# Hybrid pooling and gating layer on eight cores: the first tile's transposed input made on chip, and loads and stores issued at other places

## The reference, cut to what matters

```python
# x: (32, 2048, 1024) float32
proj = einsum('bsd,dc->bsc', x, w_in)            # 512 pool columns | 512 u | 512 v
xp = proj[..., :512]
zg = gelu(proj[..., 512:])
pooled = causal_multiscale_pool(xp)              # 4 groups, trailing means over 2/4/8/16, minus x_t
pool_out = einsum('bsgc,gcd->bsgd', pooled, pool_w) * pool_scale
sgu_out = u * (W_s @ layer_norm(v) + b_s)        # chunks of 128 positions, lower-triangular W_s, 4 heads
mix = einsum('bsc,cd->bsd', concat(pool_out, sgu_out), w_out)
h = layer_norm(alpha * x + mix)
y = layer_norm(alpha * h + (silu(h @ w_gate) * (h @ w_up)) @ w_down)   # d_ff 2816
```

## Time and profile before

| | us |
|---|---|
| three runs | 2450.92, 2452.18, 2657.8 |
| their median | 2452.18 |
| the profiled execution's own time | 2450.96 |
| its span on the slowest core (core 3) | 2449.4 |
| spans of the eight cores | 2441.9 to 2449.4 |
| PE busy on that core | 2408.5 (98%) |

### The profile page before, as it was taken

How to read it: one execution, slowest core, us unless ns; L and a number is a source line. 1 busy time by engine, 2 the same in 40 slices (tenths; PEclk the granted TensorE clock), 3 DMA queues, 4 the chain that set the end, 5 groups by cost and what they waited for, 6 DMA issues and landing times.

```text
span 2449.4 us, 33772 instructions; the slowest of 8 cores (2441.9 to 2449.4 us)
## 1 busy us (share of the span) xinstructions
PE 2408.5 (98%) x11415; PEld 1101.7 (45%) x11415; DVE 1488.9 (61%) x2348; ACT 410.0 (17%) x676; POOL 184.3 (8%) x348
## 2 busy tenths in 40 slices
PE   6999999999999999999999999999999999999997
PEld 2444444444444444444444444444444444444443
DVE  4864656647476474855647566475764747656454
ACT  1311112112121111211202111121111212112010
POOL 4211010000000000000000000000100000000000
PEclk9999999999999999999999999999999999999999
DMA  9999996555644555454555545565445564544553
GB/s 173 174 171 201 214 218 194 165 155 189 142 162 145 163 173 154 156 160 141 180 147 172 155 138 172 150 194 139 151 155 156 184 150 160 153 149 164 155 189 104
DMA packets 162393, 401.99 MB, mean 164 GB/s; under 512 B 67088, under 2 KB 67216, under 8 KB 160176
## 3 DMA queue, kind: packets, MB, share of 16 engines
q1 hardware_dynamic: 93312, 331.39, 40.9%
q0 software_dynamic: 14000, 54.80, 13.7%
q10 hardware_dynamic: 54912, 13.64, 3.6%
HBM read 386.31 MB, written 50.86 MB: 178 GB/s over the span
## 4 chain that ended last, share of the span: by engine, by line
PE 96%; DVE 2%; issue 1%; DMA 1%; POOL 0%; ACT 0%; DVEq 0%; POOLq 0%; ACTq 0%
PE ps L672 25%; PE ps L675 25%; PE ps L778 24%; PE ps L605 8%; PE ps L494 4%; PE ps L571 4%; PE ps L451 4%; DMA sb_wv<-wv 1%; PE ps L548 1%; DVE sb_lnst L231 0%; PE ps L376 0%; PE ps L643 0%; DVE sb_hr L614 0%; DVE sb_hr L249 0%; DVE sb_hr L246 0%
## 5 line engine op out<-in xcount | busy, mean ns | idle before, releaser
L672 PE MATMUL ps<-sb_hT,sb_ring 128*128 128x512 bf16 x2816 | 665.2, 379 | 0.3 <-DVE sb_aT L689 0.3
L675 PE MATMUL ps<-sb_hT,sb_ring 128*128 128x512 bf16 x2816 | 665.2, 379 | 0.0
L778 PE MATMUL ps<-sb_ring,sb_aT 128*128 128x512 bf16 x2728 | 592.7, 379 | 1.2 <-DVE sb_aT L689 1.2
L675 PEld LDWEIGHTS ps<-sb_hT,sb_ring 128*128 128x128 bf16 x2816 | 275.5, 98 | 332.3
L672 PEld LDWEIGHTS ps<-sb_hT,sb_ring 128*128 128x128 bf16 x2816 | 275.2, 98 | 332.1 <-issue 1.3
L778 PEld LDWEIGHTS ps<-sb_ring,sb_aT 128*128 128x128 bf16 x2728 | 266.5, 98 | 321.5 <-issue 1.7
L686 DVE SCALAR_TENSOR_TENSOR sb_silr<-sb_silr,ps 128x512 f32<-128x512 f32 x352 | 241.3, 686 | 278.5 <-ACT sb_silr L684 278.1
L791 DVE SCALAR_TENSOR_TENSOR sb_hr<-sb_hr,ps 128x512 f32<-128x512 f32 x124 | 76.9, 682 | 450.7 <-PE ps L778 450.7
L684 ACT ACTIVATE sb_silr<-ps 128x512 f32<-128x512 f32 x352 | 207.2, 594 | 857.0 <-PE ps L675 673.4
L689 DVE SCALAR_TENSOR_TENSOR sb_aT<-sb_silr,ps 128x512 bf16<-128x512 f32 x352 | 242.0, 688 | 63.8 <-DVE sb_silr L686 61.2
L241 POOL TENSOR_TENSOR sb_lnst<-sb_lnst,sb_mhalf 128x1 f32<-128x1 f32 x191 | 111.5, 584 | 1647.5 <-DVE sb_lnst L238 1647.4
(11 more groups left out here) (86 smaller groups left out, 1034.6 us busy)
## 6 DMA issues: line engine op xcount, KB each, us to landing
sb_ring<-scr_gu SPq DMA_DIRECT2D x315, 512.0 KB, 4.6
sb_ring<-scr_dn SPq DMA_DIRECT2D x144, 512.0 KB, 4.1
out<-sb_hr SPq DMA_DIRECT2D x63, 512.0 KB, 3.0
sb_hr<-x SPq DMA_DIRECT2D x60, 512.0 KB, 6.8
sb_ring<-w_gate_up POOLq DMA_DIRECT2D x37, 512.0 KB, 12.9
sb_xT<-xT POOLq DMA_DIRECT2D x15, 1024.0 KB, 10.1
scr_gu<-sb_ring SPq DMA_DIRECT2D x22, 512.0 KB, 9.8
sb_ring<-w_down POOLq DMA_DIRECT2D x16, 512.0 KB, 13.3
```

The source lines that it names most:

```text
L672: ins = t.matmul(ps[:, bg, :], lhsT=ring[:, s, 256 * k:256 * k + 128], rhs=hT[:, k, :], start=(k == 0), stop=(k == 7))
L675: ins = t.matmul(ps[:, bu, :], lhsT=ring[:, s, 256 * k + 128:256 * k + 256], rhs=hT[:, k, :], start=(k == 0), stop=(k == 7))
L778: ins = t.matmul(ps[:, bd[b], :], lhsT=aT[:, k, b * 128:(b + 1) * 128], rhs=ring[:, s, 512 * kk:512 * kk + 512], start=(k == 0), stop=(k = ...
```

## The change

- Tile 0's `xT` is no longer loaded. The four row blocks of x and the identity are the first loads; `xT_first` casts each block to bf16 on ACT, transposes it with eight PE instructions and copies it from PSUM into `xT` on DVE. The names `xT0` to `xT3` now stand for blocks of 128 tokens and not for pairs of planes.
- Tile 0's pool windows are recorded behind `load_xT(1)` and the first seven ring loads; their small first-16-position steps go from POOL to DVE (tile 0 alone).
- All four U of tile 1 are recorded ahead of the first slot, among the last transposes; before, they stood in slots 0 to 3.
- `issue_to` is called twice for a slot: ahead of it without cast loads (it stops at the first one), and behind the slot's posts with them.
- The output store of a block (`it_store`) is recorded two slots behind its layer norm.

```diff
-        def load_xT(mt, k0=0, k1=8):
+        def load_xT(mt):
             if mt < NMT:
-                S.dma("pool", xT[:, k0:k1, :], xT_d[mt, :, k0:k1, :],
-                      writes=[f"xT{k // 2}" for k in range(k0, k1, 2)])
+                S.dma("pool", xT[:], xT_d[mt], writes=[f"xT{b}" for b in range(4)])
...
-        def issue_to(n):
+        def issue_to(n, casts=True):
             while issued[0] < min(n, NMT * NS):
                 mt, i = divmod(issued[0], NS)
+                if from_f32(mt, i) and not casts:
+                    break
...
         def prologue():
+            S.dma("pool", ident[:], ident_d, writes=["ident"])
+            for gb in range(4):
+                load_x(gb, "pool")
             for q in range(4):
-                load_xT(0, 2 * q, 2 * q + 2)
                 S.dma("pool", wv[:, 2 * q:2 * q + 2, :], wv_d[:, 2 * q:2 * q + 2, :], writes=[f"wv{q}"])
...
-            S.dma("pool", ident[:], ident_d, writes=["ident"])
-            for gb in range(2):
-                load_x(gb, "pool")
             S.dma("pool", g1B[:], g1B_d, writes=["g1B"])
             S.dma("pool", b1B[:], b1B_d, writes=["b1B"])
-            for gb in range(2, 4):
-                load_x(gb, "pool")
...
+        def xT_first():
+            for b in range(4):
+                S.task("act", lambda a, b=b: a.activation(out=hbr[:, b, :], in_=hr[:, b, :], func=AF.Copy),
+                       reads=[f"h{b}"], writes=[f"hb{b}"])
+                bk = bank()
+                pv = ps[:, bk, :].bitcast(BF16)
+
+                def f(t, b=b, pv=pv):
+                    for k in range(8):
+                        ins = t.transpose(pv[:, k * 128:(k + 1) * 128], hbr[:, b, k * 128:(k + 1) * 128], ident[:])
+                    return ins
+                S.task("pe", f, reads=[f"hb{b}", "ident"], excl=[bn(bk)])
+                S.task("dve", lambda v, b=b, pv=pv: v.tensor_copy(
+                    out=xT[:, :, b * 128:(b + 1) * 128], in_=pv.rearrange("p (k t) -> p k t", k=8)),
+                    excl=[bn(bk)], writes=[f"xT{b}"])
...
                 if first:
-                    S.task("pool", lambda v, src=src: v.tensor_tensor(out=pC[:, g, :], ...
+                    eng = "pool" if mt else "dve"
+                    S.task(eng, lambda v, src=src: v.tensor_tensor(out=pC[:, g, :], ...
-                    S.task("pool", lambda v: v.tensor_tensor(out=mixT[:, g, 0:16], ...
+                    S.task(eng, lambda v: v.tensor_tensor(out=mixT[:, g, 0:16], ...
...
             for b, it in enumerate(ln2):
                 fill[1 + 2 * b].append(it)
+                fill[3 + 2 * b].append(it_store(4 * (mt - 1) + b))
...
                     for h in range(4):
-                        fill[h].append(it_u(1, h, early=True))
                         fill[4 + h] += [it_s(1, h), rest(ctx["u", 1, h])]
...
-                issue_to(mt * NS + j + RING - 1)
-                run_slot(fill[j] + [it_gu(j, slot_of[mt, j])])
+                issue_to(mt * NS + j + RING - 1, casts=False)
+                run_slot(fill[j] + [it_gu(j, slot_of[mt, j])])
+                issue_to(mt * NS + j + RING - 1)
                 keep(mt, j)
...
+        xT_first()
         bks = v_first()
...
         for g in (3, 2, 1, 0):
-            run_slot([it_p(0, g)])
+            run_slot([it_p(0, g, early=True)])
         load_xT(1)
         issue_to(RING)
+        for g in (3, 2, 1, 0):
+            run_slot([rest(ctx["p", 0, g])])
...
-        for it in (O[0], O[1], N[0], P[3], P[2], O[2], P[1], N[1], P[0], T[0], V[0], O[3], V[1], N[2], T[1],
-                   V[2], N[3], V[3], T[2], T[3]):
+        for it in (O[0], O[1], N[0], P[3], P[2], O[2], P[1], N[1], P[0], T[0], V[0], O[3], V[1], N[2], T[1],
+                   V[2], V[3], N[3], T[2], U[0], U[1], T[3], U[2], U[3]):
```

More of the change, by code:

```diff
@@ L365, in f @@
                         return ins
-                    S.task("pe", f, reads=[XT[q], WV[q]], writes=[bn(bks[b])] if q else (),
+                    S.task("pe", f, reads=[XT[b], WV[q]], writes=[bn(bks[b])] if q else (),
                            excl=() if q else [bn(bks[b])])
@@ L530, in windows @@
                 if first:
-                    S.task("pool", lambda v, src=src: v.tensor_tensor(out=pC[:, g, :], in0=src[:, 16:32],
+                    eng = "pool" if mt else "dve"
+                    S.task(eng, lambda v, src=src: v.tensor_tensor(out=pC[:, g, :], in0=src[:, 16:32],
                                                                      in1=icf[:, g, :], op=ALU.mult),
                            reads=[sn, "icf"], writes=[f"pC{g}"])
-                    S.task("pool", lambda v: v.tensor_tensor(out=mixT[:, g, 0:16], in0=pC[:, g, :], in1=xp[:, g, 16:32],
+                    S.task(eng, lambda v: v.tensor_tensor(out=mixT[:, g, 0:16], in0=pC[:, g, :], in1=xp[:, g, 16:32],
                                                             op=ALU.subtract),
@@ L699, in post, with it_store @@
                 ln_apply(r, hr[:, hs, :], g2B[:], b2B[:], f"h{hs}", "g2B", "b2B")
+            return None, post, 0
+        def it_store(gb):
+            def post():
+                hs = gb % H_RING
                 out_toks.append(S.dma("sp", out_d[gb * 128:(gb + 1) * 128, :], hr[:, hs, :], reads=[f"h{hs}"]))
@@ L766, in ffn @@
             for c, (half, kg) in enumerate(chunks[:NG] if last else chunks):
-                issue_to(mt * NS + NJ + c + RING - 1)
+                issue_to(mt * NS + NJ + c + RING - 1, casts=False)
                 if kg == 0:
@@ L806, in ffn @@
                 run_slot(fill[NJ + c] + [(pe, post, 0)])
+                issue_to(mt * NS + NJ + c + RING - 1)
                 keep(mt, NJ + c)
@@ L915, in build_nc @@
         T = [it_t(0, b) for b in range(4)]
+        U = [it_u(1, h, early=True) for h in range(4)]
         for it in (O[0], O[1], N[0], P[3], P[2], O[2], P[1], N[1], P[0], T[0], V[0], O[3], V[1], N[2], T[1],
-                   V[2], N[3], V[3], T[2], T[3]):
+                   V[2], V[3], N[3], T[2], U[0], U[1], T[3], U[2], U[3]):
             run_slot([it])
```

## The result

The changed kernel takes 2457.2 us (median of 14 executions, 2456.14 at best) against 2452.1 us for the kernel before in the same job (2450.76 at best). Ratio 1.0022, 95% interval [1.0013, 1.0031]: slower by about 5 us, small (the forecast's "the same" reached to 2%) but outside its own uncertainty, where 2445.5 us with a range of 2440 to 2453 was forecast.

The account below looks back on a forecast made before the run. PE's matmuls bound tiles 2 to 15. Core 3: 2449.4 - 1.9 (start, pool steps, U) - 5.7 + 1.5 (casts) = 2443.3; slowest about 2443.8, plus run overhead gives 2445.5 us, range 2440 to 2453.

Parts of the forecast that it names:

- The bound and the steady tiles: Tiles 2 to 15 are bound by PE's own matmuls, so the change gains nothing there.
- Cast loads behind the posts: -5.7 us on core 3, +1.5 given back: Tile 1: the inverse root's stall goes, gaining 5.7 us; load waits ending tiles 0 and 1 return 1.5 us.
- over 3 us of waits for ring loads at the ends of tiles 0 and 1: Sign that would show the forecast wrong: PE waiting that long there.
- The leads of 2.0 and 0.8 us: Time by which weights land before use: 2.0 us at tile 0's chunk 10, 0.8 at tile 1's chunk 11.
- Rival 1: Loads are the bound; PE's 7 us lead is paid back at tile 1's chunk 11: 2450 us, chance 0.17.
- Rival 4: Late cast loads starve the ring, 5 us at tile 0's chunk 10: 2456 to 2461 us, chance 0.13.
- Rival 2: Tile 1's stall moves to a later inverse root, about half stays: 2448.5 us, chance 0.10 shared with another rival.
- Start up to P of tile 0: From launch to tile 0's pool projection: +1.0 us, between -0.5 and +3, with V ending at 23.2 us.
- Small pool steps on DVE: Tile 0's eight 16-column instructions moved from POOL to DVE: +0.6 us, bounds 0 and +1.5.
- xT and ring ahead of the windows, U ahead of slot 0: Tile 1's P stops waiting, first gate matmul at about 90.6 us; with start and pool steps a 1.9 us gain.
- the 93 that the prediction named as a sign of being wrong: The forecast is wrong if the first gate matmul starts after 93 us.
- Output stores: Output stores recorded two slots behind their layer norm: 0 us, since PE never idles from tile 2 on.

Follow-up runs that it names:

- e16: Kernel before, with bf16 copies of seven gate and up chunks stored in tile 2 instead of tile 1, casts ahead of the posts: ratio 0.9998 [0.9976, 1.0020].
- e17: Kernel before, with GpSimd's inverse root replaced by a VectorE subtraction in tiles 0 and 1, no load moved: 2454.82 us, ratio 1.0010.
- e2: Kernel before, with only the cast loads put behind the slot's posts: 2457.79 us, ratio 1.0021.
- e7: Changed kernel, with cast loads behind the posts in tile 1 alone: 2457.75 us, ratio 1.0024.
- e9: Kernel before, with cast loads behind the posts only in slots 12 to 19 of tile 1: 2454.78 us, ratio 1.0016.
- e8: Changed kernel, with cast loads behind the posts in tile 0 alone: 2454.26 us, ratio 1.0013.
- e18: Changed kernel, with half of each weight chunk cast in tile 1 left out, same instruction order: 2449.1 us, ratio 0.9987.
- e3: Changed kernel, with tile 0's xT loaded in pieces as before: ratio 1.0025 [1.0014, 1.0036].
- e1: Changed kernel, with cast loads ahead of the posts again: 2453.77 us, ratio 1.0005.
- e15: Kernel before, with seven gate and up chunks' bf16 copies moved to tile 2 and casts behind the posts in slots 12 to 19 of tile 1: 2447.43 us.
- e11: Kernel before, with GpSimd's inverse root replaced by a VectorE subtraction everywhere, no load moved: 2457.65 us, ratio 1.0021.
- e10: Changed kernel, with cast loads behind the posts only in slots 12 to 19 of tile 1: ratio 1.0025 [1.0001, 1.0048].
- e4: Changed kernel, with the four U of tile 1 back in slots 0 to 3: 2460.64 us, ratio 1.0043.

## Why the prediction was wrong

**The bound and the steady tiles: right.** Tiles 2 to 15 did not move, and the idle time of 300 to 345 us went.

**The step that failed is "Cast loads behind the posts: -5.7 us on core 3, +1.5 given back".** The 5.7 us did go. What came back was sized at 1.5 us; with tile 0's waits aside it was 8.0 us of idle time between 345 and 400 us on core 1 and 2.9 us of lower clock behind the longest wait: tile 1 took 163.0 us there against 157.7 on core 3 before. The prediction's own sign of being wrong, over 3 us of waits for ring loads at the ends of tiles 0 and 1, came. The leads of 2.0 and 0.8 us were read, but taken as a margin. With e16 and e17 in hand they read otherwise: the later core's loads kept up only because PE stood still for 5.7 us ahead of them. POOL's wait of 22.09 us for a store was a wait on this stream of loads and stores, not a queueing accident ahead of the inverse root. Rival 1 (loads are the bound, 2450) had this mechanism, and the argument against it, that core 2 ran the stretch 7 us earlier on the same loads, does not hold: the same transfers took longer on core 3 (medians from 240 to 345 us: 12.2 us a kept store against core 2's 10.3, 11.9 a bf16 ring load against 7.2), and so it is in every pair. By e17 supply alone gives 3 to 5 us of waits; that the late issue gives the rest is argued from e2, e7 and e9, not shown apart. The lower clock behind a long wait was not in the sum at all.

**Rival 4 named the outcome (2456 to 2461), but not the place.** It had the ring starve at tile 0's chunk 10 with 5 us; PE waited 0.4 us there on core 1, and by e8 and e18 tile 0 alone costs 1 to 4 us. It was set aside because 14 us to land is more than the 10.2 us of the xT load, but the prediction's own row of a cast load shows 16.5 us for one, and on core 1 one took 17.2 us at 185.66. From 320 us on core 1's cast loads did land within 5 to 13 us of their issue; but they could not be issued until a store was done. Rival 2 (the stall moves to a later inverse root) did not come: PE idles 0.1 us between 300 and 345 us on core 1.

**Start up to P of tile 0: right in kind, mis-sized.** +1.0 was taken and -0.5 to +3 allowed. V ended at 24.3 to 26.2 and not 23.2: it started at 15.1 to 16.7 us, behind its first weights (14.4 in the sum), and its 32 matmuls took 8.3 to 10.0 us (8.8). P of tile 0 came 3.3 us later on core 1 than on core 3 before, and 4.1 us later on core 3, beyond the +3 allowed. Against e3 the part costs 2.0 us at the first gate matmul on the mean of the cores. The Trainium skill's price ("TensorE: Matmul & The Clock Gate", Part 4: about 275 ns a transpose in a kernel) is not what was missing: eight in 1.01 us are 0.13 us each.

**Small pool steps on DVE: +0.6, as far as it can be read.** From P of tile 0 to the last 36 matmuls are 15.7 us on core 0 and 16.6 on core 1 (15.8 before), so -0.1 to +0.8.

**xT and ring ahead of the windows, U ahead of slot 0: the mechanism right, the gain not.** P of tile 1 waited for nothing and took 7.07 us, and core 0 had its first gate matmul at 90.36 us (90.6 forecast). Cores 1, 3 and 5 had theirs at 93.3 to 94.1, past the 93 that the prediction named as a sign of being wrong; from the last 36 matmuls on core 1 took 31.9 us as core 0 did (31.7 in the sum), so its lateness comes from the start. But tile 0 got only 4.3 us shorter for three U of 5.2 us: PE now waits 0.8 us there for a spatial product (107.2 us). Start and tile 0 together are 224.7 us on core 3 and 223.7 on core 2 before, 227.3 on core 1 and 223.5 on core 0 after. So -1.9 became -0.2 on an early core and +2.6 on the one that counts.

**The sum.** Core 1 after against core 3 before: start +5.9 (93.3 to 87.4), tile 0 -3.4 (134.0 to 137.4), tile 1 +5.3 (163.0 to 157.7). That is 7.8 of the 8.4 us by which the spans differ; the rest was not traced.

**Output stores: 0,** as forecast as far as e1 shows it: with the pool steps and the rest they sum to 1.0005. They were not run alone.

## What to carry to other kernels

A stall on an engine that waits for a store or a load can be the place where an overfull stream of transfers is paid for; before taking the stall away, check whether the chain of waits behind it runs through DMA, and whether the leads of the next loads stay near zero. If so, cut or spread the bytes first (here seven of 34 chunks kept one tile later; 0.23% less time in e15, and the same times in six of e16's eight executions). Moving instructions only moved the wait here, and a long wait cost a lower clock on top. Where the slowest core sets the time, size a change by what it gives to the slowest core, not to the mean: here one core of each pair lost it all.

## What the runs showed that was not expected

**Cores come in pairs, and one of each loses.** In 108 executions of the kernel before the spans of cores 0 and 1, 2 and 3, 4 and 5, 6 and 7 differ by 6.3 us (median) and by more than 2 us in 429 of 432 pairs; which of the two is later changes from run to run (the odd core in 231 pairs of 432). The median of the earlier core is 2441.9 us and of the later 2448.2; with the change 2442.6 and 2453.8; with e15 2442.3 and 2443.9. What the change, e2, e3, e7 and e9 cost fell nearly all on the later cores (medians 2451.6 to 2453.8 us, the earlier ones 2441.8 to 2443.2). Their transfers land later: from 240 to 345 us, before, a kept store took 11.8 to 12.2 us (medians) on the four later cores and 10.3 to 11.1 on the four earlier ones. That the two of a pair share something on the way to DRAM fits, but was not tried apart.

**The store of a kept chunk is the slow link.** 512 KB take 12.7 us (median, core 1 of the change, 240 to 345 us) while a cast load of 1 MB f32 takes 8.8 us beside it; with half the cast bytes it is 7.6.

**A long wait can cost twice.** In the stretch from 345 to 400 us the granted clock was 0.94 on core 1 of the change (longest wait 4.58 us), core 1 of e9 (4.87) and core 3 of e7 (4.43), 0.97 on cores 4 and 6 of e9 (3.9 and 4.1), and 1.00 on all cores whose longest wait was 2.1 us or less. Between these it went either way: 1.00 on core 7 of the change (2.97) and core 6 of e11 (2.96), 0.94 on core 2 of e10 (3.31), 0.97 on core 2 of e7 (2.28), whose eight matmuls behind the wait took 3.48 us and not 1.89. So the length of the wait alone doesn't tell it. Nor does the sum of the waits: 6.9 us in four waits went with 1.00 on core 4 of e4, 8.1 us in four with 0.94 on core 1 of the change.
